# Sigmoid of each gate chunk in three steps, norm scaling as a step of its own, and two staging buffers in turn

## What is computed

```python
h = _rmsnorm(x, ln_g);  z = h @ w_in          # fq fk fv ff fg gq gk gv glr gg ma mb
# GLA, in chunks of 64 tokens, one state S (128 x 256) for each head
q_in = qc * jnp.exp(b);  k_in = kc * jnp.exp(-b)
att = jnp.where(causal, einsum('bhtd,bhsd->bhts', q_in, k_in), 0.0)
o = einsum('bhts,bhsv->bhtv', att, vc) + einsum('bhtd,bhdv->bhtv', q_in, S)
S = jnp.exp(b_last)[..., None] * S + einsum('bhsd,bhsv->bhdv', kc * jnp.exp(b_last - b), vc)
# merge
a = (o_fox.reshape(B, L, FOX_WIDTH) * jax.nn.silu(fg)) @ w_up_a
o_gla = _rmsnorm(o_gla, gla_norm_g).reshape(B, L, GLA_VW)
b = (o_gla * jax.nn.silu(gg)) @ w_up_b
m = jax.nn.sigmoid(ma) * a + jax.nn.sigmoid(mb) * b
return x + m @ w_out
```

## Time and profile before

| | us |
|---|---|
| median of 3 runs | 1828.0 |
| lowest and highest | 1827.0 and 1829.68 |
| the profiled execution | 1815.63 |
| its span, first to last instruction | 1813.9 |

### The profile page before, as it was taken

The page is one execution under the profiler, slowest core; times in us unless marked ns, Lnnn a source line. Parts: engine busy times, 40 slices in busy tenths (PEclk is TensorE's granted clock), DMA queues, the critical chain, the costliest instruction groups (busy, mean ns, idle before and its releaser), DMA issues. The chain is left out here.

```text
span 1813.9 us, 35678 instructions
## 1 busy us (share of the span) xinstructions
PE 1564.8 (86%) x11525; PEld 1304.4 (72%) x11525; DVE 689.7 (38%) x1513; ACT 621.1 (34%) x1319; POOL 493.4 (27%) x935
## 2 busy tenths in 40 slices
PE   3597979889669898899988999999987748999998
PEld 2494858778458676688766887768755548888887
DVE  5326153442643444534445344453443112333211
ACT  5135242434422434324343244442433225111111
POOL 0042332423262134233332333443140012111000
PEclk7699999999979999999999999999998879999999
DMA  4111212212055376667666666776655542322143
GB/s 130 46 47 25 81 32 60 51 53 59 14 155 168 112 225 213 208 189 211 209 201 205 198 199 203 222 228 192 200 162 165 170 179 93 141 96 85 50 117 113
DMA packets 154692, 249.72 MB, mean 138 GB/s; under 512 B 37321, under 2 KB 63434, under 8 KB 153954
## 3 DMA queue, kind: packets, MB, share of 16 engines
q1 hardware_dynamic: 122978, 215.78, 38.2%
q0 software_dynamic: 31552, 31.96, 6.6%
HBM read 217.40 MB, written 30.22 MB: 137 GB/s over the span
## 5 line engine op out<-in xcount | busy, mean ns | idle before, releaser
L280 PE MATMUL psum<-h_hi,w_hi 128*128 128x384 f32 (+1 forms) x1536 | 555.5, 362 | 62.5 <-issue 31.7
L280 PE MATMUL psum<-h_hi,w_lo 128*128 128x384 f32 (+1 forms) x1536 | 511.8, 333 | 0.0
L280 PE MATMUL psum<-h_lo,w_hi 128*128 128x384 f32 (+1 forms) x1536 | 511.3, 333 | 0.0
L280 PEld LDWEIGHTS psum<-h_hi,w_hi 128*128 128x128 f32 x1536 | 296.7, 193 | 130.2 <-issue 117.0
L1239 POOL DMA_DIRECT2D sc<-tmp_bias x512 | 252.6, 502 | 304.4 <-PE psum L1674 300.6
L280 PEld LDWEIGHTS psum<-h_lo,w_hi 128*128 128x128 f32 x1536 | 297.6, 194 | 3.0
L280 PEld LDWEIGHTS psum<-h_hi,w_lo 128*128 128x128 f32 x1536 | 296.0, 193 | 0.0
L579 POOL DMA_DIRECT2D lfk<-in_cache_logf x256 | 136.9, 535 | 259.1 <-issue 259.1
L1643 PE MATMUL psum<-con,k_page 128*128 128x128 f32 x1024 | 154.6, 277 | 32.8 <-DVE k_t L1168 22.2
L1643 PEld LDWEIGHTS psum<-con,k_page 128*128 128x128 f32 x1024 | 121.9, 142 | 53.8 <-issue 49.2
L1293 ACT ACTIVATE k_t<-psum 128x512 f32<-128x512 f32 x128 | 75.9, 593 | 201.0 <-PE psum L1643 200.8
(11 more groups left out here) (242 smaller groups left out, 2003.1 us busy)
## 6 DMA issues: line engine op xcount, KB each, us to landing
k_page<-in_cache_k SPq DMA_DIRECT2D x256, 256.0 KB, 3.5
v_page<-in_cache_v SPq DMA_DIRECT2D x256, 256.0 KB, 3.1
w_raw<-in_w_tiles SPq DMA_DIRECT2D x64, 512.0 KB, 4.6
g_pair<-tmp_gates SPq DMA_DIRECT2D x16, 544.0 KB, 4.6
sc<-tmp_bias POOLq DMA_DIRECT2D x512, 16.0 KB, 2.9
tmp_gates<-tm POOLq DMA_DIRECT2D x24, 192.0 KB, 3.5
tmp_ogla<-gate POOLq DMA_DIRECT2D x4, 1088.0 KB, 5.9
g_pair<-tmp_ogla SPq DMA_DIRECT2D x8, 544.0 KB, 4.9
```

What stands on the lines that cost most here:

```text
L280: m = pe.matmul(out, wt[:, s, k, :], h[:, k, t0:t0 + w], start=(k == 0 and a == 0), stop=(k == KT_ - 1 and a == 2))
```

## The change

The sigmoid of a gate chunk becomes three steps: "evac" (ScalarE's Abs, Exp, Ln), "ev_y" (VectorE's y, ScalarE's last Exp) and "ev_z" (VectorE's multiplies, GpSimd's store). They stand behind the first, second and third part of the next chunk. VectorE's scaling of o_n becomes a step "on" (for the sampled tokens "son") between "o" and "og". All gate chunks, of G and m tiles, take two staging buffers in turn (sig_buf); ScalarE waits for the use of the chunk two before. For m tiles z_read is given in ev_y, for G tiles in ev_z, and for G0 now behind a wait on the multiply. The place of "end" (the store of a head's output) follows ev_z. The costs of the new steps are zero.

```diff
--- before.py
+++ after.py
@@ -972,14 +972,17 @@
         out, last = [], before
         for tile in run:
             for c, parts in enumerate(z(tile)):
-                out += parts[:1] + ([(("evac", *last), 0)] if last else []) + parts[1:]
+                out += parts[:1] + ([(("evac", *last), 0)] if last else [])
+                gated = last and tiles[last[0]][0] in (G0, G1, "m")
+                for k, part in enumerate(parts[1:]):
+                    out += [part] + ([((("ev_y", "ev_z")[k], *last), 0)] if gated and k < 2 else [])
                 last = (at[tile], c)
         return out, last
 
     out, states, last = [], [], None
     for i in range(GH):
-        chain = [[((name, i, t), cost) for name, cost in (("att", 0.3), ("u", 0.55), ("o", 1.0), ("og", 0.25))] for t in range(TT)]
-        sample = [(("satt", i), 0.3), (("so", i), 1.3), (("sog", i), 0.25)]
+        chain = [[((name, i, t), cost) for name, cost in (("att", 0.3), ("u", 0.55), ("o", 1.0), ("on", 0), ("og", 0.25))] for t in range(TT)]
+        sample = [(("satt", i), 0.3), (("so", i), 1.3), (("son", i), 0), (("sog", i), 0.25)]
         extra = {(V0, 1, 0): [(("decay", i, 0), 0.7)], (V0, 1, 2): [(("decay", i, 1), 0.7)], (V0, 2, 0): [(("decay", i, 2), 0.7)],
                  (V0, 2, 2): [(("dec_last", i), 0)], (GQ, 0, 3): [(("vturn", i, 1, 2), 0.44), (("dec_neg", i), 0)],
                  (GQ, 1, 1): [(("dec_diff", i), 0)], (GQ, 1, 3): [(("dec_end", i), 0)]}
@@ -1004,11 +1007,11 @@
         if i < GH - 1:
             out += mix([x for t in range(3, TT) for x in chain[t]] + sample, body)
         else:
-            cut = next(k for k, (step, _) in enumerate(body) if step == ("evac", at[G1, i], 2))
+            cut = next(k for k, (step, _) in enumerate(body) if step == ("ev_z", at[G1, i], 2))
             out += mix([x for t in range(3, TT) for x in chain[t]] + sample, body[:cut])
             out += mix(body[cut:], [(("sstate", i, r), 0.55) for r in range(NHB)])
         states = [(("sstate", i, r), 0.55) for r in range(NHB)]
-    return out + [(("evac", *last), 0)]
+    return out + [((name, *last), 0) for name in ("evac", "ev_y", "ev_z")]
 
 
 def schedule():
@@ -1029,7 +1032,7 @@
     steps += [step for step, _ in gla]
     order = tile_order()
     for i in range(GH):
-        last = max(k for k, step in enumerate(steps) if step == ("sog", i) or step[0] == "evac" and order[step[1]] in ((G0, i), (G1, i)))
+        last = max(k for k, step in enumerate(steps) if step == ("sog", i) or step[0] == "ev_z" and order[step[1]] in ((G0, i), (G1, i)))
         steps.insert(last + 1, ("end", i))
     return steps
 
@@ -1046,8 +1049,8 @@
 
         wa = sb(ctx, "wa", [P, DK])
         ba = sb(ctx, "ba", [P, 1])
-        t1 = sb(ctx, "t1", [P, 384])
-        tm = sb(ctx, "tm", [P, 384])
+        sig_buf = [sb(ctx, f"sig{s}", [P, 384]) for s in range(2)]
+        t1 = sig_buf[0]
         kdec = sb(ctx, "kdec", [P, NT])
         q_in = sb(ctx, "q_in", [P, NT])
         k_in = sb(ctx, "k_in", [P, NT])
@@ -1102,12 +1105,21 @@
         k_in_page = [sem(f"k_landed{r}") for r in range(NK)]
         v_in_page = [sem(f"v_landed{r}") for r in range(NV)]
         sc_in = [sem(f"sc_in{r}") for r in range(SLOTS)]
-        vn_in, wa_in, pg_in, st_out, og_out, m_out, zero_set, qbd_zero, pt_zero, wa_zero = (sem(n) for n in
-            ("vn_in", "wa_in", "pg_in2", "st_out", "og_out", "m_out", "zero_set", "qbd_zero", "pt_zero", "wa_zero"))
+        vn_in, wa_in, pg_in, st_out, og_out, zero_set, qbd_zero, pt_zero, wa_zero = (sem(n) for n in
+            ("vn_in", "wa_in", "pg_in2", "st_out", "og_out", "zero_set", "qbd_zero", "pt_zero", "wa_zero"))
+        m_out = [sem(f"m_out{s}") for s in range(2)]
         stream.phase(TT * 2, 0, (0, 1))
         steps = schedule()
         tiles = tile_order()
         at = {tile: n for n, tile in enumerate(tiles)}
+        sig_order = [(n, c) for n, tile in enumerate(tiles) if tile[0] in (G0, G1, "m") for c in range(3)]
+        sig_at = {chunk: k for k, chunk in enumerate(sig_order)}
+        stores = [[k for k, (n, c) in enumerate(sig_order) if tiles[n][0] == "m" and k % 2 == s] for s in range(2)]
+
+        def sig(n, c):
+
+            return sig_buf[sig_at[n, c] % 2][:, 0:CHUNKS[c][1]]
+
         m_count = {tile: k for k, tile in enumerate(tile for tile in tiles if tile[0] == "m")}
 
         def W(eng, name, i, k):
@@ -1262,20 +1274,21 @@
                     for j in range(2):
                         pool.dma_start(outs["gla_s"][0, r + NHB * j, i], s0[:, r + NHB * j, :]).then_inc(s1_out[r], 16)
 
-                def evac(n, c):
+                def gate_out(n, c):
                     kind, x = tiles[n]
                     if kind == "m":
                         t0, w = CHUNKS[c]
                         W(pool, "m_sig", m_count[tiles[n]], c + 1)
-                        pool.dma_start(gates[x, :, t0:t0 + w], tm[:, 0:w]).then_inc(m_out, 16)
+                        pool.dma_start(gates[x, :, t0:t0 + w], sig(n, c)).then_inc(m_out[sig_at[n, c] % 2], 16)
 
                 def end(i):
                     W(pool, "gated", i, GTS)
                     W(pool, "g_mul", i, 6)
                     pool.dma_start(scratch["ogla"][i], gate[:]).then_inc(og_out, 16)
 
-                run(pool, {"prep": prep, "vn_load": vn_load, "att": att_step, "satt": satt, "sstate": sstate, "evac": evac, "end": end})
-                pool.wait_ge(m_out, 16 * 3 * len(m_count))
+                run(pool, {"prep": prep, "vn_load": vn_load, "att": att_step, "satt": satt, "sstate": sstate, "ev_z": gate_out, "end": end})
+                for s in range(2):
+                    pool.wait_ge(m_out[s], 16 * len(stores[s]))
                 pool.wait_ge(st_out, GH * 16)
                 pool.wait_ge(og_out, GH * 16)
                 for r in range(NHB):
@@ -1376,6 +1389,17 @@
                     if c == 0 and part == 1:
                         stream.split_hi(act, 0, n)
 
+                def wait_sig(eng, n, c):
+
+                    k = sig_at[n, c] - 2
+                    if k < 0:
+                        return
+                    kind, i = tiles[sig_order[k][0]]
+                    if kind == "m":
+                        eng.wait_ge(m_out[k % 2], 16 * (stores[k % 2].index(k) + 1))
+                    else:
+                        W(eng, "g_mul", i, 3 * (kind - G0) + sig_order[k][1] + 1)
+
                 def evac(n, c):
                     kind, i = tiles[n]
                     w = CHUNKS[c][1]
@@ -1383,15 +1407,23 @@
                         e = 3 * (kind - G0) + c
                         act.wait_ge(stream.projected, stream.chunk(0, n, c))
                         W(act, "dc_y", i, 3)
-                        W(act, "g_mul", i, e)
-                        sigmoid_act(act, lambda name: W(act, name, i, e + 1), inc, stream.bank_of(n, c), t1[:, 0:w])
+                        wait_sig(act, n, c)
+                        sigmoid_act(act, lambda name: W(act, name, i, e + 1), inc, stream.bank_of(n, c), sig(n, c), split=True)
                     if kind == "m":
                         x = m_count[tiles[n]]
                         act.wait_ge(stream.projected, stream.chunk(0, n, c))
-                        if 3 * x + c:
-                            act.wait_ge(m_out, 16 * (3 * x + c))
+                        wait_sig(act, n, c)
                         sigmoid_act(act, lambda name: W(act, "m" + name[1:], x, c + 1), lambda m, name: inc(m, "m" + name[1:]),
-                                    stream.bank_of(n, c), tm[:, 0:w])
+                                    stream.bank_of(n, c), sig(n, c), split=True)
+
+                def ev_y(n, c):
+                    kind, i = tiles[n]
+                    w = CHUNKS[c][1]
+                    if kind == "m":
+                        x = m_count[tiles[n]]
+                        sigmoid_act_end(act, lambda name: W(act, "m" + name[1:], x, c + 1), lambda m, name: inc(m, "m" + name[1:]), sig(n, c))
+                    else:
+                        sigmoid_act_end(act, lambda name: W(act, name, i, 3 * (kind - G0) + c + 1), inc, sig(n, c))
 
                 def ostat(i, t):
                     W(act, "o_mm", i, t + 1)
@@ -1403,7 +1435,7 @@
                     inc(A(ost[:, 2:3], ost[:, 1:2], ACT.Exp, scale=-0.5), "sr_set")
 
                 run(act, {"qbd": qbd, "kt": kstep, "pt": pstep, "pn": pn, "exp": exp, "out": out, "decay": decay, "dec_last": dec_last,
-                          "dec_neg": dec_neg, "dec_end": dec_end, "vturn": vturn, "kturn": kturn, "z": z, "evac": evac, "o": ostat,
+                          "dec_neg": dec_neg, "dec_end": dec_end, "vturn": vturn, "kturn": kturn, "z": z, "evac": evac, "ev_y": ev_y, "o": ostat,
                           "so": lambda i: ostat(i, TT)})
 
             @block.vector
@@ -1539,26 +1571,38 @@
                         W(dve, "ed_set", i, 1)
                         inc(T(k_in[:, t0:t0 + w], zb, k_in[:, t0:t0 + w], ALU.mult), "kin_set")
```

(30 more changed lines are left out.)

## The result

| | before | after |
|---|---|---|
| median of 6 runs each, us | 1827.5 | 1802.7 |
| lowest and highest | 1813.7 and 1831.4 | 1793.1 and 1808.1 |
| the profiled execution (span) | 1815.6 (1813.9) | 1803.0 (1801.3) |

The ratio is 0.9871, with a 95% interval of 0.9839 to 0.9903. That is 24 us saved, between 18 and 29. So the sign and the range held, and the saving was larger than the sum said. The profiled execution of before lies 12 us under its median, that of after on its own. So the two traces differ by only 12.6 us of span. The GLA stage, from its first projection matmul to the first of the merge, shrank from 960.9 to 943.1 us, by 17.8. The merge is equal (338 us each), and the stage of after begins 4.8 us later, which comes from the stages ahead of it that the change doesn't touch.

The account below looks back on a forecast made before the run. TensorE, busy 86% of the span, was taken as the bound, with about 56 us of waits to win. Gains of 22.9 us less costs of 5.5 gave 17.4 net: from 1828.0 to 1811 us, range 1797 to 1829.

Parts of the forecast that it names:

- (a): TensorE's 11.0 us of o_n stalls: a separate norm step widens the gap from o to og, saving 8.6 us.
- (f): Tighter gaps in the rest of the chain, att to u and u to o, cost 2.5 us (bounds 0 and 5.1).
- (g): The two projection PSUM banks are freed later; mostly hidden, costing 1 us (bounds 0 and 26).
- (b): Five k_t copy stalls behind a sigmoid or the single staging buffer, 9.6 us together: 8.3 us saved.
- (c): Four q_sp stalls, 4.0 us, from VectorE being late after G1's sigmoid and the norm: 2.5 us saved.
- (d): The long stall at 610.72 (5.05 us) behind four softmax Exps on ScalarE: 1 us saved.
- (e): The granted clock, 0.66 after the 3.57 us stall, should not fall without it: 2.5 of 3.4 us saved.
- (h): The same k_t copies meet other neighbours as steps shift; fresh collisions cost 2 us (range -2 to +6).
- Late banks: Rival: VectorE's multiply ends too late for the projection banks, 1.5 us for each of 24 chunks: 1847 us; chance 0.10.
- Loads set the pace: Rival: with TensorE faster, page loads become late and half the gain turns into v_page or k_page waits: 1819 us; chance 0.16.
- Moved, not removed: Rival: copies wait as long behind other work, so TensorE's waits stay near 56 us: 1828, give or take 3; chance 0.12.
- More than I count: Rival: nearly all o_n, q_sp and chain stalls go, half the other k_t stalls too, no fresh costs: 31 us, 1797; chance 0.12.

Follow-up runs that it names:

- spacing and no move: The changed kernel with its list entries "on" and "son" kept, but VectorE's scaling made back in "o" and "so": 1799.4 us, 0.9847 of the kernel before.
- the gates alone: The changed kernel without the entries "on" and "son", scaling in "o", sigmoids in three steps with two buffers: 1799.0 us, 0.9869 of before.
- the new entries alone: The kernel before plus empty entries "on" and "son" that only respace the chain, and the wait on G0's multiply: 1831.4 us, 1.0044 of before.

## Why the prediction was right, and where it was not

**The total** was right in sign and range, and 7 us short of the medians' difference. In the two traces the stage is 17.8 us shorter, almost the 17.4 of the sum, and that is in part luck. (a) missed 7.4 of its 8.6 us. What filled the hole is that the costs (f) and (g), 3.5 us, do not show, and that waits which the sum doesn't name, for s, pn_t and sc_new, fell from 4.9 to 0.4 us.

**(a) The o_n stalls, -8.6: failed.** They went from 11.0 to 9.8 us: from 6.2 to 3.5 in heads 0 to 2, where all were to go, and from 4.8 to 6.3 in head 3. The step of the working that failed is the sentence that a gap of 2.5 quarters "covers the Square, Ln, Exp and o_n". It covers ScalarE's part. But o_n itself is an instruction in VectorE's queue, and a later place there put it behind w_lo or y, which wait for ScalarE in turn. I had asked whether the statistic would be ready, not whether VectorE would be free. With spacing and no move the waits are 4.7 us; the move adds 5.1. In time neither shows beside the cut sigmoids (0.9869 without both, 0.9847 with the spacing, 0.9873 with both), and on top of uncut sigmoids the whole norm step costs 22 us.

**(b) k_t behind the chain, -8.3: right.** Matched transpose by transpose, the five stalls that I had counted went from 9.6 to 1.0 us, so by 8.7; the one that stayed is that at 1165.30 (0.96 of its 1.15). With the gates alone they fell by 7.9. The rest of the 12.6 us by which k_t fell is the stall of 3.9 that changed its name, smaller ones that went, and two fresh ones against them. Four that lie behind the softmax and other work (2.63, 1.70, 1.59 and 1.78 us) are the same to 0.01 us. **(c) q_sp, -2.5:** all 4.0 are gone in the whole change. **(d) The stall at 610.72, -1:** it is at 615.17 now, in a stage that begins 4.8 us later, and 4.4 us long instead of 5.05, so 0.7. **(e) The clock, -2.5:** the stretch of 0.66 is gone. Summed over the stretches of 20 us ahead of the tail, (1 - clock) x 20 us is 8.4 us before and 6.8 after, so 1.6 and not 2.5, since a short drop came up at another stall (751 us).

So the gates alone gave 24 us (19 to 29), against 14.3 us of (b) to (e). The stalls of their head sum to about 34 us, and 3 us on o_n follow behind the mark, where before had 56: some 19 us. The other 5 are not placed.

**(f) The tighter chain, +2.5:** state and att rose by 3.6 us, which looks like the term, but 3.7 of it are the stall that changed its name; the others sum to 5.0 against 5.1. Beside the cut sigmoids no run shows this cost (0.9847 with the spacing, 0.9869 without). Without the cut sigmoids the same spacing costs 8 us (4 to 12).
**(g) Late banks, +1:** no wait of the projection for a bank in the whole change. From the end of the G multiply to the reuse of its bank the 24 chunks had at least 0.85 us (before 0.68). The upper bound of 26 us in the prediction is a slip: 24 chunks at 0.56 and half of it again are 20 us. It is not in the sum. In the kernel with the gates alone six chunks just touch, with 1.1 us of waits in all. That the room was tight but sufficient is what the row at 1187 had shown.
**(h) Fresh collisions, +2:** the stall of 5.1 us on o_n at 1368 (before 0.5) and two on k_t (1.2 more at 1167 and 1.5 more at 1298) are new, smaller ones went. The first belongs to (a) as much as here, so the term can't be told apart.

**The rivals.** *Late banks* fell: even with the steps a quarter later the total stays (0.9877), though 6.7 us of bank waits then appear. *Loads set the pace* fell for the head, where no DMA wait appears. The tail is 10.4 us longer than before, and that looks like a gain given back. But the kernel with three steps and one buffer each has a head as long as before (864.8) and its tail is longer by 7.0 all the same; in all kernels with four value buffers whose chain is cut at ev_z the tail has 102.5 to 106.4 us, in all that are cut at evac 96.0 to 97.6. So most of it is work of head 3 that the new place of the cut moves across my mark, and some 3 us may be something that the loads took. I had predicted the tail unchanged without seeing that the cut moves work into it. *Moved, not removed* fell: 56 us became 39. *More than I count* comes nearest to the size of the gain, for another reason than it gave: not o_n, but the sigmoids.

Two rules that the prediction weighed can be settled. The Trainium skill (PSUM — Partial Sum Buffer, its summary of rules for kernel authors) advises prompt evacuation; here release one to two quarters later cost nothing (the room between read and reuse of the 24 G chunks fell from 5.4 to 2.4 us at the median), so in this kernel lateness had no price until the next writer was due. It also says (VectorE: DVE Perf Modes, rules for kernel authors) that for chained VectorE operations their number counts and not the semaphores; here the number is equal in both kernels, 1513, and the time is 24 us apart. The rule speaks of a chain on one engine, and this one runs between two that work in order. The measurement decides.

**What stays open.** Whether the second buffer is needed for the m tiles, for the G tiles or for both: only the wait for the store of an m chunk shows in the trace, but the two were not tried apart. Which stalls of the gates' part stand for which us was not tried one by one. Whether the place of the scaling is worth 0 or 5 us beside cut sigmoids is below what five rounds tell.

## What to carry to other kernels

When a chain goes back and forth between two engines that work in order, cut it into steps with other work between and give it a second buffer in the same edit: here either alone was worth 5 us or nothing, both 24. Before a step is moved later, look at what stands ahead of it in that engine's queue at the new place and what that waits for; time for its inputs is only half of the question. And when a stream waits for loads at the end of a stage, look for buffers whose own stream has ended: five of them brought another 24 us here.

## What was not expected of the hardware

**The clock adds to a stall, and not always.** The kernel with the new entries alone has almost the same stalls around 720 us as the kernel before (2.12 and 1.54 us there, 1.92 and 1.40 before), yet its granted clock falls there and that of before does not. In the second stretch it has a stall of 1.97 us (at 863) that before lacks. First the new entries alone, then before:

```profile
720.00:740.00 20.00, 18.45 (x142) 14.74 (x141) 8.79 (x28) 7.30 (x18) 0.47 (x1) 0.83 0.44 143
...
860.00:880.00 20.00, 18.03 (x136) 13.66 (x134) 9.10 (x22) 8.20 (x20) 1.53 (x3) 0.91 0.61 190
```

```profile
720.00:740.00 20.00, 18.60 (x159) 14.23 (x157) 10.86 (x33) 8.32 (x20) 0.90 (x2) 1.00 0.58 177
...
860.00:880.00 20.00, 19.72 (x179) 15.90 (x178) 8.40 (x24) 6.99 (x17) 5.71 (x12) 1.00 0.63 194
```

Each drop is time at the lower of the two levels, 1.2 instead of 2.4 GHz. Between 560 and 1380 us the sum of (1 - clock) x 20 us is 19 us there, 17 with the norm step alone, 19 with three steps and one buffer, and 8 before. So some 10 us of the difference in these traces is clock and not waiting: part of the price of a stall is paid after it. In the faster kernels the sum is 8 to 13. The stall of 2.63 us before one key transpose is the same before (at 754.0) and after (at 751.3); from 750 to 760 us the clock is 1.00 before and 0.83 after. Why one stall of about 2 us is followed by a drop and another isn't, these runs don't show.

**The spread of one kernel.** The runs of the kernel before on one chip went from 1813.7 to 1832.5 us (17 runs), 1%, and one profiled execution of it lay at the low end. A difference between two traces can be off by as much as the effect looked for. Here the traces showed 12.6 us and the medians 24.8.
